# Down projection of a hybrid decoder layer: three steps of the load and copy order moved

## The reference

```
p = rmsnorm(x) @ w_in                  # 5120 columns; two mixers: gated chunk mixing, gated short convolution
x = x + concat(groupnorm(y_a), groupnorm(y_b)) @ w_out
h = rmsnorm(x)
gate, new_ffn = causal_dwconv(h @ w_gate, ffn_prev, conv_ffn_w, conv_ffn_b)   # 5632 columns
x = x + (silu(gate) * (h @ w_up)) @ w_down                                   # 5632 -> 2048
y = rmsnorm(x)
```

## Time and profile before

| | us |
|---|---|
| runs | 2309.63, 2309.39, 2306.58 (median 2309.39) |
| profiled execution | 2307.53 |
| its span, first to last instruction | 2305.9 |
| TensorE matmuls busy | 2265.4 (98%) |
| VectorE busy | 1655.2 (72%) |
| ScalarE busy | 1014.6 (44%) |
| GpSimd busy | 504.1 (22%) |
| granted clock, mean | 0.993 |

### The profile page before, as it was taken

One profiled execution on the slowest core, in us unless ns is written; L12 is line 12 of the kernel. 1 busy time (PEld: TensorE's weight loads), 2 busy tenths in 40 slices (PEclk: granted clock), 3 DMA queues, 4 the chain that ended last, 5 costly groups with the idle time before them and its releaser, 6 DMA issues. The chain is left out here.

```text
span 2305.9 us, 44056 instructions
## 1 busy us (share of the span) xinstructions
PE 2265.4 (98%) x16978; PEld 2253.8 (98%) x16978; DVE 1655.2 (72%) x2237; ACT 1014.6 (44%) x1599; POOL 504.1 (22%) x599
## 2 busy tenths in 40 slices
PE   7999999999999999999999999999999999999996
PEld 7999999999999999999999999999999999999996
DVE  6347754545422676888888888888888798888885
ACT  6224321213211353444454444545444565555575
POOL 2310000000222101111111111111112356655574
PEclk9999999999999999999999999999999999999998
DMA  7322232223533244453444435344446566775432
GB/s 243 98 76 71 75 90 76 83 80 85 183 117 94 73 142 121 128 165 119 152 134 140 150 119 165 123 146 138 136 157 214 179 230 217 235 231 200 173 93 101
DMA packets 369228, 320.15 MB, mean 139 GB/s; under 512 B 8680, under 2 KB 348771, under 8 KB 363616
## 3 DMA queue, kind: packets, MB, share of 16 engines
q1 hardware_dynamic: 346464, 203.98, 30.2%
q0 software_dynamic: 22656, 114.69, 13.4%
HBM read 258.32 MB, written 60.31 MB: 138 GB/s over the span
## 5 line engine op out<-in xcount | busy, mean ns | idle before, releaser
L1892 PE MATMUL ps<-h_hi,w_hi 128*128 128x288 f32 x1728 | 513.1, 297 | 0.0
L1894 PE MATMUL ps<-h_hi,w_lo 128*128 128x288 f32 x1728 | 509.3, 295 | 0.0
L1893 PE MATMUL ps<-h_lo,w_hi 128*128 128x288 f32 x1728 | 509.2, 295 | 0.0
L2251 PE MATMUL ps<-form,dw_hi 128*128 128x288 f32 x1232 | 365.9, 297 | 3.7 <-DVE dw_lo L1790 2.6
L2252 PE MATMUL ps<-form,dw_hi 128*128 128x288 f32 x1232 | 362.6, 294 | 0.0
L2253 PE MATMUL ps<-form,dw_lo 128*128 128x288 f32 x1232 | 362.0, 294 | 0.0
L1892 PEld LDWEIGHTS ps<-h_hi,w_hi 128*128 128x128 f32 x1728 | 324.7, 188 | 0.8
L1893 PEld LDWEIGHTS ps<-h_lo,w_hi 128*128 128x128 f32 x1728 | 324.7, 188 | 0.1
L1894 PEld LDWEIGHTS ps<-h_hi,w_lo 128*128 128x128 f32 x1728 | 324.5, 188 | 0.0
L1288 DVE TENSOR_TENSOR w_lo<-raw,w_hi 128x1024 fp32r<-128x1024 f32 x128 | 163.0, 1302 | 198.4 <-ACT w_hi L799 198.1
L1790 DVE TENSOR_TENSOR dw_lo<-down,dw_hi 128x512 fp32r<-128x512 f32 (+1 forms) x282 | 242.5, 866 | 73.6 <-ACT dw_hi L813 73.0
(11 more groups left out here) (298 smaller groups left out, 5258.2 us busy)
## 6 DMA issues: line engine op xcount, KB each, us to landing
raw<-in_w_gate_dram SPq DMA_DIRECT2D x88, 512.0 KB, 4.3
raw<-in_w_in_dram SPq DMA_DIRECT2D x80, 512.0 KB, 4.3
down<-in_w_down_dram SPq DMA_DIRECT2D x32, 1024.0 KB, 5.4
form<-act_scratch POOLq DMA_DIRECT2D x28, 1152.0 KB, 6.8
act_scratch<-stage POOLq DMA_DIRECT2D x46, 576.0 KB, 4.4
raw_c<-in_w_up_dram SPq DMA_DIRECT2D x40, 512.0 KB, 3.8
raw_d<-in_w_up_dram SPq DMA_DIRECT2D x40, 512.0 KB, 5.0
raw<-in_w_out_dram SPq DMA_DIRECT2D x32, 512.0 KB, 3.9
```

What stands on the lines that cost most here:

```text
L1892: te.matmul(out, whi, xhi, start=start, stop=False)
L1893: te.matmul(out, whi, xlo, start=False, stop=False)
L1894: return te.matmul(out, wlo, xhi, start=False, stop=stop)
L2251: te.matmul(out, dw_hi[:, m % 4, j, :], act_f[:, j, 0, :], start=start and j == 0, stop=False, skip_group_check=True)
```

## The change

Three edits. One: the load of form 6 of chunks 1 to 5 leaves the last visit of the chunk before, and stands in the chunk's first visit, behind the addition of the second snap and ahead of the sums; what it waits for is the same. Two: forms 7 and 8, both issued in visit 1 before, are issued in visits 1 and 2. Three: the copies of the state rows (`rows_stage`) stand behind the first high half of visit 3, not ahead of it.

```diff
@@ GpSimd, loop over the visits
                 if v >= VISITS:
                     snap_add(v, 1, p5_snap, 2 * gv + 1, 1)
+                if ch >= 1 and gv == 0:
+                    pool.wait_ge(down_landed[(v + 1) % 2], 16 * ((v + 1) // 2 + 1))
+                    load_form(NQ * ch + 6, piece_done, D0 + NQ * (v - 1) + 2)
                 if v + 1 < VISITS * len(CHUNKS):
                     sums13(v + 1)
...
-                if v == 1:
-                    for k in (7, 8):
-                        load_form(k, piece_done, N_LAST + 5)
+                if v in (1, 2):
+                    load_form(v + 6, piece_done, N_LAST + 5)
                 elif 3 <= v <= 5:
                     load_form(v + 6, lo_ready, D0 + 2 * NQ)
...
                 if ch < len(CHUNKS) - 1 and gv == VISITS - 1:
-                    for t in (5, 6):
-                        if t == 6:
-                            pool.wait_ge(down_landed[(v + 2) % 2], 16 * ((v + 2) // 2 + 1))
-                        load_form(NQ * (ch + 1) + t, piece_done, D0 + NQ * v + t - 4)
+                    load_form(NQ * (ch + 1) + 5, piece_done, D0 + NQ * v + 1)
@@ ScalarE, loop over the visits
                 bank_snap(v, 2, 3, bank_a, u2_snap)
-                if v == 2:
-                    rows_stage()
                 if v in LATE_ROUNDS:
                     act_hi(PAIRS - 1, LATE_ROUNDS[v])
                 more = v + 1 < VISITS * len(CHUNKS)
                 if more:
                     down_hi(m + 7)
+                    if v == 2:
+                        rows_stage()
                     down_hi(m + 8)
-                if more:
                     down_hi(m + 9)
```

## The result

| us | before | after |
|---|---|---|
| median of 7 runs each | 2308.17 (2306.58 to 2311.38) | 2316.16 (2315.45 to 2318.07) |
| profiled execution | 2307.53 | 2315.90 |
| its span | 2305.9 | 2314.3 |

The ratio is 1.0036 [1.0027, 1.0046]: slower by 0.36%, which is more than a measurement of this kernel can leave in doubt. The forecast was no measurable change, 2311.0. That did not come; the time lies inside the range (2307 to 2317), 5 us above the likeliest value and near the upper end.

The account below looks back on a forecast made before the run. TensorE was taken as the bound, busy 2265.4 of 2305.9 us. Terms -1.1, 0, 0 and +3.4 gave +2.3: 2309.8 from the profiled execution, 2311.7 from the median; forecast 2311, range 2307 to 2317.

Parts of the forecast that it names:

- B: TensorE's 1.12 us wait in visit 3, before 1810.35: spreading two form loads would remove it, gaining 1.1 us.
- State rows: Copies moved behind a high half near visit 3: cost 0, up to 0.6 us if the weights still landed at 1803.0.
- part 1: Spreading the two form loads of visit 1 over visits 1 and 2: gain 1.1 us, bounds 0 and 1.3.
- C: TensorE's 1.5 us wait in visit 8, ending with a low half at 1857.16: unchanged by the later form load, cost 0.
- D to G: Last-form loads of visits 16, 24, 32 and 40, in that order: issued later, they make TensorE wait, +3.4 us.
- D: Visit 16, seventh product: the last form's load, taken as 5.6 us, makes its start 0.9 us later.
- E: Visit 24, seventh product: the last form's load, taken as 5.8 us, makes its start 1.0 us later.
- G: Visit 40, seventh product: the last form's load, taken as 5.4 us, makes its start 0.7 us later.
- rival in which they would land in time: Late loads of visits 16, 24, 32 and 40 cause no waits: -1.1 us, 2308.3 from the median; chance 0.17.
- part 3: Each chunk's last form loaded behind an addition: cost 0 at visit 8, +3.4 us at visits 16, 24, 32 and 40.
- as slow as before: Late loads at visits 16 to 40 stay slow, crowded by weights loads: +6.8 us in all, 2316.2; chance 0.15.
- a granted clock of 1.00 in these stretches: Sign the forecast was right: the clock stays full around the form waits of visits 16, 24, 32 and 40.

Follow-up runs that it names:

- e5: The kernel before with the loads of forms 7 and 8 spread over visits 1 and 2, nothing else: 2305.64 us, ratio 0.9990.
- e8: The kernel before with only the state row copies moved behind the first high half of visit 3: 2306.89 us, ratio 0.9994.
- e6: The kernel after with each chunk's last form issued behind the fifth's load, one visit earlier, without its wait for weights: 2305.53 us, ratio 0.9990.
- e9: The kernel after with the last form's issue moved behind the two sums: 2345.26 us, ratio 1.0161.
- e4: The kernel after with GpSimd waiting, behind the last form's issue, for VectorE's low half of the seventh product: 2311.20 us, ratio 1.0020.
- e7: The kernel after with the load of form 28 put off from visit 24 to visit 29: 2310.22 us, ratio 1.0012.
- e3: The kernel after with only form 27, read in visit 24, loaded in its old place: 2308.16 us, ratio 1.0004.
- e8b: The kernel before with only the state row copies moved, profiled a second time: visit 3 waits 0.67 us.
- e8c: The kernel before with only the state row copies moved, profiled a third time: visit 3 waits 1.05 us.
- e2: The kernel before with only the load of each chunk's last form moved behind the first GpSimd addition: 2318.10 us, ratio 1.0044.

## Why the prediction was right, and where it was not

**B, -1.1.** Right. The wait is gone, in e5 too, and the weights of visit 3 took 6.8 us where I said about 7.1.

**State rows, 0.** Right, as far as e8 can tell. But "This edit lives on part 1" is not borne out: no cost showed without part 1 either.

**C, 0.** Right in size: 1.47 became 1.38. The issue went out at 1850.24, took 4.7 us, and the form alone is now the releaser. e6 shows what C hung on: the wait for the weights ahead of the issue, not the 4.4 us of the load.

**D to G, +3.4.** Right in mechanism, low in size. The loads took 5.7, 6.4, 5.8 and 5.4 us where I took 5.6, 5.8, 5.5 and 5.4. Less what was late before (0.18 at D, 0.2 at E), the waits are +1.2, +1.4, +0.9 and +0.6 = +4.1. G's 5.3 us before was not measured "with both neighbours": the weights went out at 2191.69, after the form had landed at 2191.48, so the load had only the other form load beside it and stood nearer to an undisturbed one than the prediction says. With 5.3 everywhere E is +0.5 and the sum +2.3, not +2.2, which changes nothing. The rival in which they would land in time, and the fit of the Trainium skill (DMA: Bandwidth & Descriptors, section "Anatomy of one DMA — SWDGE (gpsimd) path") with 4.0 and 4.7 us for the two sizes, fall: the shortest of the five moved loads were 4.7 us for 864 KB and 5.4 for 1152 KB.

**The step that failed** is the last sentence of part 3: "The issue that now stands between the addition and the next sums holds these up by 0.55 us at E to G; VectorE has that and more while TensorE waits, so nothing is added." I costed the issue by its own length, on GpSimd, and asked whether the sums could bear it. What it did was to take away VectorE's turn between them. e9 shows the turn back when the issue is elsewhere, e4 shows that with the low half ahead the weights are in time, e7 shows that the crowd at 2014 is the other half, and e3 that this one issue carries nearly all. At D, F and G the hold is in the trace as well (4.14, 4.12 and 4.12 us for two low halves, from 1920.76, 2108.06 and 2198.06) and nothing waits behind it: at D and F only one form load goes out beside the weights, without the residual's, and these take 7.8 and 7.6 us. In the profile: 4.3 us of new waits in visit 26, and up to 1.7 us more from the clock. The sign "a granted clock of 1.00 in these stretches" held at D and E and failed here: it was 0.83 over these 10 us, and 0.66 from 2041 to 2046. The window of the kernel after for 2035 to 2045, in which the kernel before had 1.00:

```profile
2035.00:2045.00 10.00, 6.33 (x35) 6.15 (x36) 9.17 (x9) 2.19 (x4) 5.28 (x6) 0.83 0.89 308
```

The sum, made again for the profiled execution: 2309.8 predicted, +0.7 (D to G), -0.1 (C), -0.2 (less wait in visit 0), +4.3 (visit 26), +1.7 (clock, at most: 0.17 of 10 us) = 2316.2, against 2315.90.

The rows had the warning. The earlier trace rows is a low half held for 4.30 us, right behind the issue of C, and I used it only to say that the hold would go at visit 8 (it became 3.0 us). Asking why VectorE was held there, when a low half of that size takes 0.56 us elsewhere, and where else the change makes that order, would have given the hold at D to G. The rival "as slow as before" named the time that came, 2316.2, for another reason: its loads of 6.5, 8.0 and 6.8 us did not come. That the time fell inside the range is luck in this sense: the upper end stood for slow loads, and what filled it was the chain of visit 26, which no rival named.

Left open: why the kernel of e4 spreads so widely, why the form wait of visit 0 varies from 0 to 1.7 us between executions of one kernel (e8, e8b, e8c), why the clock fell behind the waits of visit 26 in the kernel after and not in e2, and what inside the two engines takes the turn away.

## What to carry to other kernels

When an instruction is moved, ask what it now stands directly ahead of, not only what it delays: here 0.55 us of issue ahead of a run of GpSimd work made a low half of VectorE 3.5 us long, and the loss came out two visits later, by way of a weights load. A low half that frees a buffer is on the path of a DMA even when no engine seems to wait for it; follow the release to the issue, and the issue to the traffic that it will meet. And before a load is moved later, try it earlier, without the wait that it stands behind: that version is 10 us faster than the later one here, though it can't be told from leaving the load where it was (e5).

## What the runs showed of the hardware

- Where a low half of VectorE fell into a run of GpSimd's sums, the two took turns: sums of 128x512 on GpSimd are 1.74 us with a low half between them and 1.31 without. Where a DMA issue on GpSimd's queue stood directly ahead of the run, the turn was not given: the low half took 3.5 us, through three GpSimd instructions. This shows at visits 8 (3.0 us, of 128x384), 16, 24, 32 and 40, and in visit 26 (4.5 us), of the kernel after, at visit 24 of e7, and at visit 8 of the kernel before (4.3 us); it is absent at visit 24 of the kernel before, of e3 and of e9, where no issue stands directly ahead of the run, and in visit 26 of e7, where 0.12 us lie between the issue and the run (1.77 us).
- The granted clock stayed at 1.00 behind a single wait of 1.6 us. Behind one of 2.6 us it was 0.66 over 5 us twice (visit 26 of the kernel after, 2041 to 2046, and 1928 to 1933 of e2) and 1.00 once (visit 26 of e2); both in visit 26 had waits of 0.6 to 1.2 and 1.1 us a few us ahead. Behind those of 5.4 to 6.5 us in e9 it was 0.50 to 0.67 over 5 us, and 0.50, at three of the five, is the 1.2 GHz level.
- Three loads issued within 0.7 us of each other took 6.6, 10.3 and 12.2 us for 576, 1152 and 1024 KB. With one of them away the 1024 KB took 9.4, and issued ahead of the others 7.4.
